# The first eight cache copies in pieces of 16320 bytes, the other eight in pieces of 4080 bytes

## What is computed

```
k_all = jnp.concatenate([cache_k_win[l].astype(k2.dtype), k2], axis=1)
...
keep_s = min(W_MAX, L_all)
ks_rows.append(k_all[:, L_all - keep_s:])
```

## Time and profile before

| | before |
|---|---|
| median of 3 runs | 3423.79 us |
| profiled execution | 3429.48 us |
| its span, first to last instruction | 3427.7 us |
| DVE busy | 2710.3 us (79%) |
| PE busy | 2561.2 us (75%) |
| POOL busy | 1256.1 us (37%) |
| ACT busy | 717.0 us (21%) |
| bytes moved by DMA | 1386.73 MB, 405 GB/s in the mean |
| HBM read, written | 1370.99 MB, 80.04 MB |

### The profile page before, as it was taken

The page is one execution under the profiler, slowest core; times in us unless marked ns, Lnnn a source line. Parts: engine busy times, 40 slices in busy tenths (PEclk is TensorE's granted clock), DMA queues, the critical chain, the costliest instruction groups (busy, mean ns, idle before and its releaser), DMA issues.

```text
span 3427.7 us, 40003 instructions
## 1 busy us (share of the span) xinstructions
PE 2561.2 (75%) x14040; PEld 1166.0 (34%) x14040; DVE 2710.3 (79%) x7309; ACT 717.0 (21%) x1565; POOL 1256.1 (37%) x1092
## 2 busy tenths in 40 slices
PE   6876597677768776777677767876787767779876
PEld 5544245322332233233323332433243322234321
DVE  5387897898898879887989798979897974345865
ACT  2210232033103310231024102420142002122110
POOL 0112223134434444444345444544444332223342
PEclk8998799898888888988889888998899778889999
DMA  9999999989999999999999999999999999999997
GB/s 332 383 410 409 399 409 363 423 354 420 421 391 396 421 421 416 405 421 417 416 396 417 421 421 396 391 421 421 406 416 416 421 412 423 418 416 400 413 407 325
DMA packets 218457, 1386.73 MB, mean 405 GB/s; under 512 B 28424, under 2 KB 39176, under 8 KB 67336
## 3 DMA queue, kind: packets, MB, share of 16 engines
q0 software_dynamic: 156672, 1140.92, 81.1%
q1 hardware_dynamic: 41040, 141.81, 10.7%
q10 hardware_dynamic: 20544, 101.45, 7.3%
HBM read 1370.99 MB, written 80.04 MB: 423 GB/s over the span
## 4 chain that ended last, share of the span: by engine, by line
DVE 40%; DMA 28%; PE 19%; issue 10%; ACT 2%; POOL 1%; ACTq 0%; POOLq 0%; DVEq 0%; SPq 0%
DMA t<-in_expert_uv,t 28%; DVE t L1101 12%; PE psum L1479 10%; DVE t L968 5%; PE psum L1381 3%; PE psum L1422 3%; DVE psum L1128 2%; DVE t L1113 2%; DVE t L1049 2%; DVE t L1047 2%; DVE t L1050 1%; DVE t L1048 1%; DVE t L992 1%; DVE t L1046 1%; DVE t L1076 1%
## 5 line engine op out<-in xcount | busy, mean ns | idle before, releaser
L647 POOL DMA_INDIRECT t<-in_expert_uv,t x1088 | 1255.9, 1154 | 2137.4 <-PE psum L1475 866.4
L1479 PE MATMUL psum<-t,t 64*64 64x512 f32 x4896 | 1343.8, 688 | 634.9 <-DVE t L1113 634.1
L1101 DVE CUSTOM_DVE_ANT_0 t<-t,t 128x1024 f32<-128x1024 f32 x1088 | 1322.2, 1222 | 483.0 <-DMA t<-in_expert_uv,t 469.7
L1479 PEld LDWEIGHTS psum<-t,t 64*64 64x64 f32 x4896 | 342.3, 148 | 1452.5 <-DVE t L1113 856.8
L1475 PE MATMUL psum<-t,t 64*64 64x512 f32 x2496 | 766.7, 743 | 0.0
L807 ACT ACTIVATE t<-t 128x2 f32<-128x2 f32 x544 | 110.9, 204 | 1853.4 <-DVE t L1101 1823.3
L1422 PEld LDWEIGHTS psum<-t,t 128*128 128x128 f32 x2304 | 277.7, 200 | 71.2 <-issue 65.0
L1422 PE MATMUL psum<-t,t 128*128 128x128 f32 (+1 forms) x2304 | 288.7, 286 | 2.6 <-ACT t L769 2.6
L1303 PE MATMUL psum<-t,t 128*128 128x128 f32 (+2 forms) x768 | 253.8, 491 | 12.4 <-DMA t<-in_xT 6.2
L968 DVE SCALAR_TENSOR_TENSOR t<-t,t,t 128x128 f32<-128x128 f32 x840 | 238.2, 346 | 0.0
L1475 PEld LDWEIGHTS psum<-t,t 64*64 64x64 f32 x2496 | 173.3, 154 | 0.5 <-issue 0.5
(11 more groups left out here) (142 smaller groups left out, 2067.2 us busy)
## 6 DMA issues: line engine op xcount, KB each, us to landing
t<-in_wq_t ACTq DMA_DIRECT2D x65, 1024.0 KB
out<-in_cache_k_win SPq DMA_DIRECT2D x8, 4080.0 KB
out<-in_cache_v_win SPq DMA_DIRECT2D x8, 4080.0 KB
t<-in_w_in_t ACTq DMA_DIRECT2D x44, 512.0 KB, 9.1
t<-in_kc_t SPq DMA_DIRECT2D x8, 2560.0 KB
t<-in_vc_t SPq DMA_DIRECT2D x8, 2560.0 KB
t<-in_expert_uv,t POOLq DMA_INDIRECT x1088
t<-in_w_v_t ACTq DMA_DIRECT2D x6, 1024.0 KB
```

Of the source, the lines that this page charges most:

```text
L647: pool.indirect_dma_start(ring[:, r, :], None, I["expert_uv"], bass.IndirectOffsetOnAxis(ap=idn[t % 2][:, s:s + 1], axis=0)).then_inc(land ...
L1101: dve.tensor_tensor_reduce(out=ring[:, r, 0:D], in0=x1[t % 2][:, :], in1=ring[:, r, 0:D], scale=1.0, scalar=0.0, op0=ALU.mult, op1=ALU.add ...
L1479: last = pe.matmul(MAIN[t][half][NS * a:NS * a + NS, :], zt[NS * a:NS * a + NS, k % Z_RING, j, :], vv[NS * a:NS * a + NS, :], start=(c == ...
```

## The change

The number of pieces is taken from the copy's index: 2 x 128 pieces of 4080 floats (16320 bytes) for copies 0 to 7, and 2 x 512 pieces of 1020 floats (4080 bytes) as before for copies 8 to 15. Nothing else is changed; the bytes, the waits and the order of issue are the same.

```diff
             def copy_cache(i):
                 new, old = ((kc_o, I["cache_k_win"]), (vc_o, I["cache_v_win"]))[i % 2]
-                sp.dma_start(new[i // 2].rearrange("t c -> (t c)").rearrange("(b a m) -> a b m", b=2, a=512),
-                             old[0, i // 2, NT:WIN].rearrange("t h e -> (t h e)").rearrange("(b a m) -> a b m", b=2, a=512)).then_inc(cache_out, 16)
+                pieces = 128 if i < PH else 512
+                sp.dma_start(new[i // 2].rearrange("t c -> (t c)").rearrange("(b a m) -> a b m", b=2, a=pieces),
+                             old[0, i // 2, NT:WIN].rearrange("t h e -> (t h e)").rearrange("(b a m) -> a b m", b=2, a=pieces)).then_inc(cache_out, 16)
```

## The result

The changed kernel took 3441.14 us in the median of six runs (3438.86 to 3445.32), the kernel before 3425.01 in the median of six. By the ratio of the runs, 1.0038, interval [1.0025, 1.005], it is some 13 us slower; the medians are 16 us apart. The forecast of next to no change (3425.5, range 3412 to 3437) was wrong. The profiled execution took 3441.22 us, its span 3439.4 us, 11.7 over that of before.

What follows compares the result with a forecast made beforehand. DMA transfers were taken to set the pace, most at the start. Terms -4.7 - 0.6 + 3 + 4.7 = +2.4 us on the profiled 3429.48, 3426 on the median; forecast 3425.5 us, range 3412 to 3437.

Steps and rivals of the forecast that it cites:

- (a): Before 131 us: longer pieces move faster while copies run nearly alone, leaving less for later; -4.7 us, ends -16 and +9.
- rival D: Slower: long pieces between DRAM tensors move slower, under 18 MB in 62 to 131 us; 3440 us, chance 0.06.
- Rival A: Faster: long pieces run at the sample-cache loads' rate before 131 us, 26 MB moved; 3412 us, chance 0.26.
- (c): Queue sharing from 131 us: turns of 1.01 us for 0.55, copies through at 177 us, contention costs +3 us, 0 to 6.
- the sentence ahead of the terms: From 62 to 350 us the 16 DMA engines are full, so time there equals work; no size of its own.
- (d): Holes in 290 to 360 us: transfers brought forward leave gathers that don't fill the engines; +4.7 us, 0 to 10.
- Rival B: Slower: gathers starve beside the copies until 186 us, 7 to 13 us behind, and don't catch up; 3434 us, chance 0.15.
- point of decision: Gather pairs after 190 us: staying near 9.5 us instead of falling below 9 means the gathers don't catch up.
- Rival C: ACT's weight loads come late through longer turns and PE waits, some 5 us added; 3430 us, chance 0.05.

## Why the prediction was wrong, point by point

(a) held. SP's queue moved 21.12 MB in 62 to 131 us; 21.3 was the value taken. 1.82 MB more at 419 GB/s are 4.3 us, for 4.7. The Trainium skill's figure for long rows that the prediction's rival D named ("DMA: Bandwidth & Descriptors", section "Latency and other measured facts") is 207 GB/s per direction for rows of 16 KiB at a pitch of 512 KiB, and 214 at 4 MiB and 4 KiB. These copies, whose pieces lie end to end, made more: 21.12 MB in 85.6% of 69 us is 358 GB/s. Rival A's 26 MB was not reached either.

The turns of (c) held, in count and in length: 300 to 300 to 298, copies through about 184 us for 177. The Trainium skill's preferred packet of at most 4096 bytes ("DMA: Bandwidth & Descriptors", section "SWDGE vs HWDGE vs iDMA"), by which the prediction had the shares stay as they were, did not show. The contention that (c) priced at +3 hardly came: 415 GB/s for 419, 0.5 us.

The step that failed is the sentence ahead of the terms, "these are full ... and time there equals work". It let me count what the engines carry and not who is waiting, so that the gathers are served last was itself priced at nothing; (c) and (d) hold only stalls and holes. In 131 to 186 us the engines lost 0.5 us of work, but the gathers lost 3.4 MB to the copies, and the ninth came 18.7 us late. From the fifth gather's issue to its landing, 135.01 to 183.65 us, the three queues were served 753, 748 and 754 packets, 47 turns an engine of 1.03 us: that is the 48.64 us of the chain. I had also taken the landing time for the pace from the start; until 155 us it was hidden behind TensorE's projections, and the change brought it out. Rival B had the gathers at 7 to 8.1 MB by 186 us and 7 to 13 us behind; they had 6.27 MB, as an engine served 36 of their pieces until 177 us (4.69 MB) for the 46 counted, and then 12 (1.57 MB) for 16, with the copies running until 184.

Term (d), which was to hold what comes after, was mis-sized: +4.7 taken, 10 the upper end. From 300 to 361 us the engines had 328 GB/s for 399: 71 x 61 us are 4.3 MB, or 10.3 us at 419. I had sized it by 500 to 550 us at 380 GB/s, where weight loads hold 25% of the engines; here they held 11%. With the 4.3 us gained in (a), 0.5 lost in 131 to 186, 0.7 lost in 186 to 260 (4 GB/s for 74 us) and 1.4 gained in 260 to 300 (15 GB/s for 40 us), the stretches give 5.8 us of the 10.3 by which the 49th gather is late. The rest would be the order of the bytes, gathers last; no run assigns it further, and it stays open.

Rival B named what happened, with a chance of 0.15: pairs stayed at 9.48 us until the copies were gone, as its point of decision had it. Its price of 11 us falls 2 short of the 13 by the ratio, 5 short of the 16 by the medians. Rival C was not the cause, but its cover is thin, as 32640 bytes showed. From the second tile on the trace follows the old one with a shift, as forecast, but the shift is 8 to 12 us, over the 7 that the prediction named as its limit.

## What to carry to other kernels

When transfers share the engines in turns of one piece, the length of a piece is its queue's weight: make it short on a queue that nobody waits for while a latency-bound queue is running, and long only where it is alone, which gained nothing here (ratio 1.0001 with copies 0 to 3). Full DMA engines don't make an exchange of order free: a queue with few buffers loses what it is denied, unless it can later run faster than its own chain allows. Before calling a reordering neutral, multiply the pieces in flight by the new turn and compare that with the wait in the chain.

## What the runs showed of the hardware

A piece is taken whole in its turn, up to 32640 bytes at least (320 packets to 321 in the row above, with 74.1% of the engines' time for the one queue and 18.1% for the other). The order of the packets shows the turns too: where the changed kernel's packets in 150 to 170 us are joined end to start, 860 of 881 steps go from the gathers' queue to SP's, from SP's to ScalarE's, or from there to the gathers'. Nearly alone, DRAM-to-DRAM pieces of 16320 bytes moved 22.4 B/ns an engine (21.12 MB in 85.6% of 16 x 69 us) against 19.8 with 4080 (19.30 MB in 88.2%), and 21.5 with 32640 (22.30 MB in 93.8%). A 4080-byte piece among others made 26.1. So the slower pace of copies running alone is mostly not a cost per piece; what it is was not tested.
